# A decoder trunk on one core: MoBA's rotary rows packed by SBUF transfers into 128 partitions

## The reference, cut to what matters

```python
def rotary(x, pos, rot_dim, theta):          # rot_dim = 32 for MoBA
    half = rot_dim // 2
    inv = theta ** (-jnp.arange(half) / half)
    ang = pos[..., None] * inv
    x1, x2, rest = x[..., :half], x[..., half:rot_dim], x[..., rot_dim:]
    return jnp.concatenate([x1 * cos - x2 * sin, x2 * cos + x1 * sin, rest], axis=-1)
```

## Time and profile before

| | us |
|---|---|
| median of 3 runs | 611.93 (611.83, 611.93, 613.43) |
| the profiled execution's own time | 613.36 |
| its span | 611.6 |
| PE, TensorE's matmuls, busy | 582.0 (95%) |
| DVE, VectorE, busy | 412.6 (67%) |
| ACT, ScalarE, busy | 379.4 (62%) |
| POOL, GpSimd, busy | 44.0 (7%) |
| the 16 DMA engines, share of queue 1 | 46.6% |

### The profile page before, as it was taken

One profiled execution on the slowest core, in us unless ns is written; L12 is line 12 of the kernel. 1 busy time (PEld: TensorE's weight loads), 2 busy tenths in 40 slices (PEclk: granted clock), 3 DMA queues, 4 the chain that ended last, 5 costly groups with the idle time before them and its releaser, 6 DMA issues.

```text
span 611.6 us, 9584 instructions
## 1 busy us (share of the span) xinstructions
PE 582.0 (95%) x3850; PEld 532.1 (87%) x3850; DVE 412.6 (67%) x618; ACT 379.4 (62%) x561; POOL 44.0 (7%) x43
## 2 busy tenths in 40 slices
PE   3999998999999999999999999999989999999984
PEld 3998997999899898889988999999879998888973
DVE  3987368636966795566657773879956962776554
ACT  5864485247257765555766747679747828565752
POOL 4001003001001000100000001105010100100000
PEclk9999999999999999999999999999989999999998
DMA  7746453445444473465335455245333553356101
GB/s 228 268 141 212 140 192 124 157 138 207 139 138 143 140 268 139 140 228 183 138 138 198 147 191 192 95 141 210 138 137 138 201 213 138 122 188 240 35 1 69
DMA packets 51871, 97.82 MB, mean 160 GB/s; under 512 B 1236, under 2 KB 7668, under 8 KB 51828
## 3 DMA queue, kind: packets, MB, share of 16 engines
q1 hardware_dynamic: 51828, 97.22, 46.6%
HBM read 96.16 MB, written 1.05 MB: 159 GB/s over the span
## 4 chain that ended last, share of the span: by engine, by line
PE 63%; DVE 16%; ACT 9%; DVEq 6%; issue 3%; ACTq 2%; DMA 1%; SPq 0%
PE proj L1527 10%; PE proj L1528 10%; PE proj L1529 10%; PE proj L1545 8%; PE proj L1547 8%; PE proj L1546 8%; DVE w_lo L936 5%; PE head L1635 4%; ACT w_hi L436 3%; PE head L1724 1%; ACT xT_hi L458 1%; DVE junk L1403 1%; DVEq L1126 1%; DVE work L1125 1%; DVE xT_lo L960 1%
## 5 line engine op out<-in xcount | busy, mean ns | idle before, releaser
L936 DVE TENSOR_TENSOR w_lo<-raw_weights,w_hi 128x1024 fp32r<-128x1024 f32 x176 | 220.5, 1266 | 140.1 <-ACT w_hi L436 138.0
L436 ACT ACTIVATE w_hi<-raw_weights 128x1024 fp32r<-128x1024 f32 x176 | 184.2, 1057 | 129.4 <-PE proj L1529 74.1
L1527 PE MATMUL proj<-xT_hi,w_hi 128*128 128x256 f32 x768 | 222.0, 289 | 2.3 <-DVE xT_lo L960 1.7
L1528 PE MATMUL proj<-xT_lo,w_hi 128*128 128x256 f32 x768 | 217.2, 283 | 0.0
L1529 PE MATMUL proj<-xT_hi,w_lo 128*128 128x256 f32 x768 | 217.2, 283 | 0.0
L1527 PEld LDWEIGHTS proj<-xT_hi,w_hi 128*128 128x128 f32 x768 | 147.1, 192 | 4.6 <-issue 3.6
L1528 PEld LDWEIGHTS proj<-xT_lo,w_hi 128*128 128x128 f32 x768 | 147.2, 192 | 0.9 <-issue 0.7
L1529 PEld LDWEIGHTS proj<-xT_hi,w_lo 128*128 128x128 f32 x768 | 147.1, 192 | 0.0
L1545 PE MATMUL proj<-w_hi,y_hi 128*128 128x512 f32 x192 | 76.2, 397 | 0.0
L1547 PE MATMUL proj<-w_lo,y_hi 128*128 128x512 f32 x192 | 74.8, 390 | 0.0
L1546 PE MATMUL proj<-w_hi,y_lo 128*128 128x512 f32 x192 | 74.8, 389 | 0.0
(11 more groups left out here) (233 smaller groups left out, 687.8 us busy)
## 6 DMA issues: line engine op xcount, KB each, us to landing
raw_weights<-in_ev_w_in_dram SPq DMA_DIRECT2D x15, 2048.0 KB, 8.5
raw_weights<-in_od_w_in_dram SPq DMA_DIRECT2D x12, 2048.0 KB, 8.0
raw_weights<-in_ev_w_out_dram SPq DMA_DIRECT2D x4, 2048.0 KB, 8.0
raw_weights<-in_xa_wkv_dram SPq DMA_DIRECT2D x4, 2048.0 KB, 8.2
raw_weights<-in_od_w_out_dram SPq DMA_DIRECT2D x4, 2048.0 KB, 7.7
raw_weights<-in_xa_wq_dram SPq DMA_DIRECT2D x2, 2048.0 KB, 9.3
raw_weights<-in_xa_wo_dram SPq DMA_DIRECT2D x2, 2048.0 KB, 8.1
raw_weights<-in_ev_w_in_dram SPq DMA_DIRECT2D x4, 512.0 KB, 5.8
```

The costliest lines, as they stand in the source:

```text
L436: act.activation(ring_quarter(w_hi, n, q), raw_quarter(n, q), ACT.Copy).then_inc(hi_ready, 1)
L936: dve.tensor_tensor(ring_quarter(w_lo, n, q), raw_quarter(n, q), ring_quarter(w_hi, n, q).bitcast(F32), ALU.subtract).then_inc(lo_ready, 1)
L1527: pe.matmul(dst, wh[:, k, :], x_hi[:, k, :], start=(k == 0), stop=False)
L1528: pe.matmul(dst, wh[:, k, :], x_lo[:, k, :], start=False, stop=False)
```

## The change

The 32 rows of four heads, which lie on partitions 0 to 31 one head beside the other, are copied into `scan_mask` so that head h lies on partitions 32h to 32h + 31: q in columns 0 to 255, k in columns 512 to 767, each with a scratch area beside it. POOL issues four transfers of 32 by 256 elements (32 KB) for that, and after the turn four transfers back (`pack`, `unpack`). `rope_moba` works on 128 partitions by 256 elements and waits for the transfers in place of the rows; a drain ahead of the shuffle is gone. TensorE's waits for `q_ready` and `k_ready` become waits for the transfers back. POOL's queue now has, for g = 0, pack q, `y_low(1)`, unpack q, pack k, unpack k, and for g = 1 pack q, `y_low(2)`, unpack q, pack k, unpack k, and then `y_low(3)`. The constants for the angles are laid out for all 128 partitions. The splits inside the rotations stay where they are.

```diff
--- before.py
+++ after.py
@@ -200,6 +200,8 @@
         k_ready = sem("k_ready")
         scores = sem("scores")
         row_max = sem("row_max")
+        rot_packed = [sem(f"rot_packed{w}") for w in range(2)]
+        rot_back = [sem(f"rot_back{w}") for w in range(2)]
         probs = sem("probs")
         probs_norm = sem("probs_norm")
         probs_turned = sem("probs_turned")
@@ -410,8 +412,31 @@
             keys_carried(0)
             y_low(0)
             keys_carried(1)
-            for i in range(1, 4):
-                y_low(i)
+
+            def pack(g, w, rows):
+
+                pool.wait_ge(rows, 2 * g + 2)
+                for h in range(4):
+                    pool.dma_start(scan_mask[32 * h:32 * h + 32, 512 * w:512 * w + S], blocks(w)[0:32, h, :]
+                                   ).then_inc(rot_packed[w], 16)
+
+            def unpack(g, w, turned_rows):
+
+                pool.wait_ge(turned_rows, g + 1)
+                for h in range(4):
+                    pool.dma_start(blocks(w)[0:32, h, :], scan_mask[32 * h:32 * h + 32, 512 * w:512 * w + S]
+                                   ).then_inc(rot_back[w], 16)
+
+            for g in range(2):
+                pack(g, 0, q_rows)
+                if g == 0:
+                    y_low(1)
+                else:
+                    y_low(2)
+                unpack(g, 0, q_ready)
+                pack(g, 1, k_rows)
+                unpack(g, 1, k_ready)
+            y_low(3)
             rg_products(0)
             y_low(4)
             rg_products(1)
@@ -1161,22 +1186,19 @@
                 ahead(z, 2)
                 ahead(z, 3)
 
-            def rope_moba(w, ready, done, cnt, n, q):
-
-                dve.wait_ge(ready, cnt)
+            def rope_moba(g, w, done, n, q):
+
                 mask = [(j + 16) % 32 for j in range(32)]
-                x32 = blocks(w)[0:32, :, :]
-                t32 = blocks(2)[0:32, :, :]
-                cos = trig[0:32, 2:3, :].broadcast_to([32, 4, S])
-                sin = trig[0:32, 3:4, :].broadcast_to([32, 4, S])
-                dve.drain()
-                dve.stream_shuffle(W[0:32, 2, :], W[0:32, w, :], mask)
+                x = scan_mask[:, 512 * w:512 * w + S]
+                t = scan_mask[:, 512 * w + S:512 * w + 2 * S]
+                dve.wait_ge(rot_packed[w], 16 * 4 * (g + 1))
+                dve.stream_shuffle(t, x, mask)
                 dve.drain()
                 ahead(n, q)
-                dve.tensor_tensor(t32, t32, sin, ALU.mult)
-                dve.tensor_tensor(x32, x32, cos, ALU.mult)
-                dve.drain()
-                dve.tensor_tensor(x32, x32, t32, ALU.add).then_inc(done, 1)
+                dve.tensor_tensor(t, t, trig[:, 3, :], ALU.mult)
+                dve.tensor_tensor(x, x, trig[:, 2, :], ALU.mult)
+                dve.drain()
+                dve.tensor_tensor(x, x, t, ALU.add).then_inc(done, 1)
 
             def softmax_max(i, h, moba):
 
@@ -1231,9 +1253,9 @@
                 ahead(k, 2)
                 if g:
                     norm_rows(1, mem_rows, mem_rows)
-                rope_moba(0, q_rows, q_ready, 2 * g + 2, k, 3)
+                rope_moba(g, 0, q_ready, k, 3)
                 ahead(v, 0)
-                rope_moba(1, k_rows, k_ready, 2 * g + 2, v, 1)
+                rope_moba(g, 1, k_ready, v, 1)
                 ahead(v, 2)
                 ahead(v, 3)
                 ahead(z, 0)
@@ -1676,8 +1698,8 @@
                 slab_f(z, [0])
                 if g:
                     pe.wait_ge(memT_ready, 4)
-                pe.wait_ge(q_ready, g + 1)
-                pe.wait_ge(k_ready, g + 1)
+                pe.wait_ge(rot_back[0], 16 * 4 * (g + 1))
+                pe.wait_ge(rot_back[1], 16 * 4 * (g + 1))
                 pe.wait_ge(y_ready, 2 + g)
                 for h in range(4):
                     pe.matmul(head[h][:, 0:P], W[:, 0, S * h:S * h + P], W[:, 1, S * h:S * h + P],
@@ -1839,9 +1861,9 @@
     ret = np.float32(10000.0) ** (-(np.arange(64, dtype=np.float32)) / np.float32(64))
     moba = np.float32(500000.0) ** (-(np.arange(16, dtype=np.float32)) / np.float32(16))
     c[:, C_INV_RET] = ret[p % 64]
-    c[:32, C_INV_MOBA] = moba[p[:32] % 16]
+    c[:, C_INV_MOBA] = moba[p % 16]
     c[:, C_SIGN_RET] = np.where(p < 64, -1.0, 1.0)
-    c[:, C_SIGN_MOBA] = np.where(p < 16, -1.0, 1.0)
+    c[:, C_SIGN_MOBA] = np.where(p % 32 < 16, -1.0, 1.0)
     c[:, C_LOG_G:C_LOG_G + 8] = np.log1p(-2.0 ** (-5.0 - np.arange(8.0)))[None, :]
     return c
 
```

## The result

| us | before | changed |
|---|---|---|
| median (runs) | 613.43 (611.83 to 615.14, 5) | 626.98 (623.61 to 627.41, 5) |
| ratio | | 1.0212, interval 1.0188 to 1.0236 |
| profiled execution, its span | 613.36, 611.6 | 623.61, 621.9 |
| VectorE busy | 412.6 | 399.2 |
| TensorE busy | 582.0 | 585.0 |

A forecast was written before the change was run, and what follows sets the result against it. TensorE, busy 95% of the span, was taken to bound the kernel. Waits for k's transfers (+15.3 us) and clock falls (+3.6 us) made +18.9 us, applied to the 611.93 us median: 631 us, range 617 to 643.

The forecast's parts named there:

- q's trips hidden: Both groups: q's packing and way back cost TensorE nothing; in group 0 packing has 4.6 us of cover.
- The sum, +18.9 us: Whole kernel: +15.3 us for the two groups' waits plus 3.6 us for clock falls.
- c: POOL's queue: price of issuing one transfer, taken as 1.0 us, with ends 0.3 and 1.3.
- L: Transfers' landing after the last of four issues, taken as 1.8 us, with ends 1.3 and 2.5.
- rival 2: POOL's issues cost a middling 0.4 to 0.65 us: waits about half, 4.5 us, 616.5 us; chance 0.09.
- rival 3: Transfers wait among weight loads, landing in 4 to 5 us on four trips: about 10 us more, 641; chance 0.10.
- The clock: TensorE's second wait in each group drops the clock for the scores: 1.8 us a group, 3.6 us in all.
- Rival 1: POOL's issues are cheap, 0.3 us: TensorE loses its waits, gains at most 1.6 us, 610.3 us; chance 0.08.
- 24c + 4L - 15.9: Both groups' chain to the scores: net delay in us, 15.3 at the values taken for issue and landing.
- Rival 5: VectorE's packed operations are not shorter: up to 13 us more, 644 us; chance under 0.02.
- the 15.3 forecast for the chain: Scores' delay through k's packing, turning and way back: +7.8 us in group 0, +7.5 us in group 1.
- The gain that I thought VectorE could give at most: MoBA stretches: a faster VectorE can give back at most some 1.6 us, TensorE's idle time there.

The follow-up runs named there:

- experiment 2: Changed kernel with SyncE holding the weight load beside k's packing until k is packed, both groups: 627.77 us, ratio 1.0243 to the kernel before.
- experiment 3: Changed kernel with VectorE's split of z's first quarter moved ahead of the wait for k's packed rows: 627.87 us, ratio 1.0234 to the kernel before.
- experiment 6: Changed kernel with only k packed and sent back, q turned on 32 partitions: 626.16 us, ratio 1.0227 to the kernel before.
- experiment 4: Changed kernel with only q packed and sent back, k turned on 32 partitions: 609.92 us, ratio 0.9946 to the kernel before.
- experiment 1: Changed kernel with POOL packing k before it sends q back: 617.29 us, ratio 1.0072 to the kernel before.
- experiment 5: The kernel with only q packed, run again beside fresh runs of the kernel before: 610.28 us, ratio 0.9955.
- experiment 7: Changed kernel with POOL packing k before sending q back, and the weight load held until k is back: 611.02 us, ratio 0.9971 to the kernel before.

## Why the prediction was right or wrong

The sign, the place and the mechanism held: q's trips hidden, k's issues behind q's way back, a wait of VectorE of 8 to 9 us (8.90 and 8.30) with the split behind it, and TensorE's first wait in each group (6.07 and 3.94 us). 631 us was forecast, 626.98 measured, inside the range. The sum, +18.9 us against +13.0, was off in three terms, of which two cancelled at one place.

- **One issue on POOL, c.** I took 1.0 us, by POOL's own middling operation and not by SP's issue. It is 0.50 us at the median and 0.66 at most. SP's rows, 0.30 and 0.84, were the nearer ones: an issue resembles an issue more than it does an elementwise operation of the same engine.
- **Landing, L.** I took 1.8 us for all trips. After the last issue's end it is 1.2 to 1.4 us alone and 5.8 (group 0) and 5.2 (group 1) beside the weight load. For k's packing I had 8c + L = 9.8 us; measured are 9.7 (154.40 to 164.14). So rivals 2 and 3 both came true, rival 3 on two of its four trips, and by luck their errors cancelled in the one step that decides. For k's way back, with no load beside it, they did not: 4c + L = 5.8 us forecast, 3.6 measured at most (167.70 to 171.28) and 3.2 (227.65 to 230.83). From k ready to the scores that makes 2.0 us less than forecast in group 0 and 2.2 in group 1.
- **The clock.** I put 3.6 us for falls that meet the scores. The clock did fall behind the first wait of each group, and quarter 0 of z ran at 0.50 (0.21 us from matmul to matmul instead of 0.12), but that quarter lay beside k's way back. In group 0 it ended at 171.3, just as the rows came: TensorE did not wait again, and the scores had the full clock. In group 1 the clock was back for the second half of the quarter, a wait of 0.33 us followed, and the scores had the full clock too. So of the two waits a group that I forecast, the second hardly came, and in the profiled execution the term is zero. I had reasoned that the first fall is hidden; I had not carried on that a slower quarter also fills the second gap, and so prevents the second fall; no run isolates that. The four executions without a trace had more of the lower clock. Of their 2.2 to 3.8 us, 1.8 may be the fall at L1657 that the profiled one lacks (the last section); whether the rest is a fall that met the scores is open. From profile to profile the change costs 10.3 us, with a fall at L1657 it would be 12.1, and the ratio says 13.0: the last microsecond of the loss stands in no trace. In experiments 2, 3 and 6, where TensorE idles ahead of the scores, they do run at the lower clock: from their first to their fourth pair of matmuls 3.49 us (experiment 2) and 3.97 us (experiment 3) instead of 1.97 us (experiment 4). So the price per fall, 1.8 us, was about right (1.5 and 2.0 here) and its place, in the trace, was not.
- **Group 0's start.** q was ready 1.1 us later than I had it (154.1), because the split at 149.85 took 3.08 us instead of the 1.96 of the earlier trace rows.
- **Rival 1** fell with c, though not by much: at 0.49 and a landing of 1.8 us the formula gives 24c + 4L - 15.9 = 3.1 us, a small loss. By the formula, then, the change would have been nearly even without the weight load. The sentence of the Trainium skill, "DMA: Bandwidth & Descriptors", section "Issuing engines are not separate DMA queues", on issues that are usually cheap was nearer to the truth (0.49 us) than my choice of c, and the sum was saved by the load. **Rival 5** is out: 0.45 and 0.42 us for the packed operations.
- The scores' shift by the trace, 12.3 us, is 3.0 us below the 15.3 forecast for the chain. Group 0 has 7.5 instead of 7.8: k landed 1.3 us later (164.14 for 162.8), was ready another 0.4 late, and its way back took 2.0 less. Group 1 has 4.8 instead of 7.5: 0.5 less up to the landing, 2.2 less on the way back.

That nothing behind the scores gives the time back held too. The gain that I thought VectorE could give at most, 1.6 us, was too low: q alone gives 1.8 to 3.4 us by the medians, and 3.2 to 3.4 from fastest execution to fastest. 1.55 us of idle were counted where the scores then moved by 2.3 us. Behind a wait the first matmul is slower as well (0.47 us at 157.59, its neighbours 0.39), which the idle time leaves out; whether that is the difference, and where the last microsecond comes from, was not tested.

## What to carry to other kernels

A transfer put in place of slow operations is priced by where its round trip stands, not by its bytes: with 6.3 to 7.8 us between the last issue and the use it was free even beside a load, and without cover four transfers of 32 KB cost more than the operations they saved. Read the issuing engine's queue as an order of its own: here a transfer whose data were ready stood behind one whose data were not. And ask what large load the same stretch releases, since small transfers issued beside it landed 4 to 6 us after the last issue instead of 1.2.

## What was not expected of the hardware

- **Small transfers beside a large load.** A 32 KB transfer lands 1.7 to 1.8 us after its issue began, 1.2 after the issue's end, when the DMA engines are free, and 4 to 6 us after the last issue when a 2 MB load runs, though it is on a queue of its own. The Trainium skill, "DMA: Bandwidth & Descriptors", section "Queues, rings and completion order", says that a DMA engine takes turns between queues packet by packet, which would let a small transfer through early. The runs don't agree with that: from the last issue to the first instruction that had waited for it were 5.1 to 6.1 us in group 0 of five kernels (the changed one and experiments 1, 2, 3 and 6), 4.4 to 5.5 in group 1, and 1.2 where the load was held. Not only the completion was late, but the data: of the packets of POOL's queue in the changed kernel, 60 moved from 156 to 160 and 160 from 160 to 164, when k's last issue was long over (158.3). k landed near the load's end, yet the end is not what frees a small transfer. q's packing in the changed kernel, issued from 139.41 to 141.55, had landed before VectorE used it at 149.33, while the loads still filled the engines up to 150:

```profile
scan_mask<-work POOLq DMA_DIRECT2D x4, 32.0 KB, 5.2
148.00:149.00 1.00, 1.00 (x10) 1.00 (x9) 1.00 (x2) 0.70 (x1) 0.00 (x0) 1.00 1.05 393
```

  What holds the packets for those microseconds was not tested.
- **VectorE's split beside POOL's subtraction.** The split that usually takes 1.2 us took 1.96 in the kernel before, where it started at 150.80, and 3.08 in the changed one, where it started at 149.85. In both it ended 1.08 us after POOL's `y_low` did (151.68 and 151.85). So it stood still until POOL was through, and starting it sooner won nothing. The Trainium skill, "SBUF — State Buffer", section "Who interferes with whom", says that a VectorE instruction with two inputs in SBUF contends with a GpSimd instruction that reads SBUF, and that one blocks wholly; the trace agrees. 1 of the 3.3 us that packing won at q went this way.
- **The clock's fall behind the same wait is not in every execution.** The wait of 2.58 us at L1635 has a fall behind it in the profiled run of the kernel before, and the same wait of 2.6 us has none in that of the changed kernel, nor in those of experiments 5 and 7 (1.00 from 447 to 455). That is the 1.8 us by which the span grew less than the scores moved. Experiments 4 and 5 are one kernel, traced twice, and show it best: with the same wait, the same 16 matmuls took 4.55 us once and 2.89 us once, and the spans were 608.6 and 607.0.

```profile
447.36 4.55 PE L1672 MATMUL head<-att,v_rows 128*128 128x256 f32 x16 [2.59 <-DVE v_rows L1474]
447.37 2.89 PE L1672 MATMUL head<-att,v_rows 128*128 128x256 f32 x16 [2.57 <-DVE v_rows L1474]
```

  The runs of the kernel before lie in two clusters, near 611.9 and near 613.6, as far apart as these two spans. That this fall separates them too is likely; the one trace of that kernel, with the fall, is of the upper cluster.
